# The gated-delta stage of a two-block network kernel: substitution rows by VectorE transposes, diagonal blocks in 32-partition squares, gates ahead of output tiles

## What is computed

```python
def gated_delta_rule(q, k, v, g, beta):          # chunks of 64 tokens, 16 value heads, 8 query/key heads
    g = jnp.cumsum(g, axis=-1)
    decay = jnp.exp(jnp.where(lower, g[..., :, None] - g[..., None, :], -jnp.inf))
    L = jnp.where(strict, jnp.einsum('bhncd,bhnsd->bhncs', kb, k) * decay, 0.0)
    T = lax.linalg.triangular_solve(eye + L, ..., lower=True, unit_diagonal=True)
    u = T @ vb
    w = T @ (kb * jnp.exp(g)[..., None])
    attn = jnp.einsum('bhncd,bhnsd->bhncs', q, k) * decay
    # scan over chunks: v_new = u - w @ state; o = q_dec @ state + attn @ v_new; state = state*g_last + k_dec^T @ v_new
```

## Time and profile before

| | us |
|---|---|
| median of 3 runs | 2825.57 (2825.46 to 2825.92) |
| the profiled execution | 2824.96 |
| its span, first to last instruction | 2822.8 |
| PE busy | 2751.5 (97%) |
| DVE busy | 1599.3 (57%) |
| ACT busy | 1206.9 (43%) |
| POOL busy | 633.0 (22%) |
| gated-delta stage with its projections | about 1885 to 2484 on the span's clock |

### The profile page before, as it was taken

The page is one execution under the profiler, slowest core; times in us unless marked ns, Lnnn a source line. Parts: engine busy times, 40 slices in busy tenths (PEclk is TensorE's granted clock), DMA queues, the critical chain, the costliest instruction groups (busy, mean ns, idle before and its releaser), DMA issues.

```text
span 2822.8 us, 40991 instructions
## 1 busy us (share of the span) xinstructions
PE 2751.5 (97%) x14276; PEld 2233.3 (79%) x14276; DVE 1599.3 (57%) x2460; ACT 1206.9 (43%) x1813; POOL 633.0 (22%) x602
## 2 busy tenths in 40 slices
PE   8999999999999999999999999998999999899998
PEld 6888887788888888887778888877888888677777
DVE  5444336544433675437945754257777777676664
ACT  4333242533332333224443332345555555457665
POOL 2000003100001450013633510113333333223222
PEclk9999999999999999999999999999999999999999
DMA  5333322233333564332214643322222222222222
GB/s 148 97 97 91 95 75 83 75 97 97 97 95 99 149 186 120 96 94 79 68 37 125 188 142 91 95 70 75 56 66 69 68 69 61 49 68 60 67 60 67
DMA packets 484837, 255.37 MB, mean 90 GB/s; under 512 B 17843, under 2 KB 478422, under 8 KB 484710
## 3 DMA queue, kind: packets, MB, share of 16 engines
q1 hardware_dynamic: 484534, 253.40, 31.4%
q10 hardware_dynamic: 176, 0.27, 0.0%
HBM read 251.51 MB, written 2.13 MB: 90 GB/s over the span
## 4 chain that ended last, share of the span: by engine, by line
PE 86%; DVE 6%; ACT 3%; issue 2%; POOL 1%; DMA 0%; ACTq 0%; DVEq 0%; POOLq 0%; SPq 0%
PE bank L258 68%; PE bank L1840 2%; DVE w_lo L244 1%; PE bank L1871 1%; PE bank L1944 1%; PE bank L1873 1%; PE bank L1872 1%; DVE dsa_work L1542 1%; ACT w_hi L238 1%; DVE small L1540 1%; PE bank L2748 1%; PE bank L2740 1%; POOL gdn_dn_off L2500 1%; PE bank L2773 1%; PE bank L946 1%
## 5 line engine op out<-in xcount | busy, mean ns | idle before, releaser
L258 PE MATMUL bank<-x_hi,w_hi 128*128 128x512 f32 x2320 | 940.7, 405 | 7.6 <-DVE w_lo L244 3.7
L258 PE MATMUL bank<-x_hi,w_lo 128*128 128x512 f32 x2320 | 907.8, 391 | 0.0
L258 PE MATMUL bank<-x_lo,w_hi 128*128 128x512 f32 x2320 | 907.0, 391 | 0.6 <-DVE x_lo L554 0.6
L244 DVE TENSOR_TENSOR w_lo<-w_raw,w_hi 128x1024 fp32r<-128x1024 f32 x429 | 547.9, 1278 | 561.5 <-ACT w_hi L238 561.1
L238 ACT ACTIVATE w_hi<-w_raw 128x1024 fp32r<-128x1024 f32 x429 | 450.6, 1055 | 612.9 <-PE bank L258 567.4
L258 PEld LDWEIGHTS bank<-x_hi,w_hi 128*128 128x128 f32 x2320 | 437.0, 188 | 104.9 <-issue 14.1
L258 PEld LDWEIGHTS bank<-x_hi,w_lo 128*128 128x128 f32 x2320 | 436.4, 188 | 93.3
L258 PEld LDWEIGHTS bank<-x_lo,w_hi 128*128 128x128 f32 x2320 | 437.5, 189 | 89.4 <-issue 5.7
L429 POOL TENSOR_TENSOR sumsq<-sumsq,sq 128x512 f32<-128x512 f32 x51 | 85.3, 1673 | 1285.8 <-ACT sq L415 1285.2
L258 PE MATMUL bank<-h_hi,w_hi 128*128 128x512 f32 x768 | 298.9, 389 | 1.6 <-DVE h_lo L1575 1.6
L258 PE MATMUL bank<-h_hi,w_lo 128*128 128x512 f32 x768 | 298.8, 389 | 0.0
(11 more groups left out here) (483 smaller groups left out, 3556.9 us busy)
## 6 DMA issues: line engine op xcount, KB each, us to landing
w_raw<-in_ffn_wi_dram SPq DMA_DIRECT2D x176, 512.0 KB, 3.8
w_raw<-in_ffn_wo_dram SPq DMA_DIRECT2D x64, 512.0 KB, 3.6
w_raw<-in_ada_w_dram SPq DMA_DIRECT2D x48, 512.0 KB, 4.9
w_raw<-in_a_w_in_dram SPq DMA_DIRECT2D x48, 512.0 KB, 4.0
w_raw<-in_b_w_in_dram SPq DMA_DIRECT2D x32, 512.0 KB, 4.1
w_raw<-in_ffn_wo_dram SPq DMA_DIRECT2D x32, 384.0 KB, 3.1
w_raw<-in_even_w_in_dram SPq DMA_DIRECT2D x16, 512.0 KB, 4.1
w_raw<-in_a_w_out_dram SPq DMA_DIRECT2D x16, 512.0 KB, 3.6
```

The source lines that it names most:

```text
L244: dve.tensor_tensor(w_lo[s][:], w_raw[raw_of(b) % RAW][:], w_hi[s][:].bitcast(F32), ALU.subtract).then_inc(w_lo_done, 1)
L258: mm = pe.matmul(out, lhs[:, w], rhs(kt), start=first and kk == 0 and m == 0, stop=last and kk == len(kts) - 1 and m == 2)
```

## The change

It touches the gated-delta stage alone.

- The selection matmuls and `pick` are gone. DVE transposes the 128 columns of C in 32 x 32 squares ("across"), then transposes a pattern that repeats each element 16 times into 1920 columns of SBUF ("rows"), which hold row k of each block spread over its partitions. The substitution reads its rows there, where it read PSUM banks.
- `m` is no longer 2 x (128 x 512) but four products of 32 partitions x 256 elements on the 32 x 32 squares of the diagonal, and the two reductions become one addition of two halves. POOL masks the decay likewise in four squares for both heads.
- The output norm is folded into the gate: POOL multiplies silu(z) by W5 ("zr", two products); DVE's `normed` goes.
- The two gates silu(z) are taken in the turn of their own projection, and the z blocks are ahead of Oa, Ob in the order of blocks; output tiles come late in a turn.
- "ga", "gb" go from DVE to ACT; DVE's `at_0`, `at_1` from ahead of the substitution to behind "f2b"; DVE's `low` from ahead of "va", "vb" to behind them; f2 waits for "hb".
- ACT's logarithms, roots, gate rows and decays of the next head run at t = 1 and 2; the table load for the logarithms stands at the turn's end. Splits, convolutions and output additions are moved as the tables say.

The diff, cut:

```diff
-            "mid": {"kt": "q0", "kk": "q1", "vt": "q2", "sel": "q3", "inv": "k0 k1 k2 k3 v00 v01 v02", "c": "v03", "f2": "v10", "v": "v11 v12", "y": "v13 O0",
-                    "at": "O1", "vn0": "O2", "ds0": "O3", "ks1": "O4", "vn1": "O5", "ds1": "O6", "ks2": "O7", "vn2": "z00", "ds2": "z01",
-                    "ks3": "z02", "vn3": "z03 z10", "o3": "z11 z12 z13"},
+            "mid": {"kt": "q0", "kk": "q1", "vt": "q2 q3", "inv": "k0 k1 k2 k3 v00 v01 v02", "c": "v03", "f2": "v10", "v": "v11 v12", "y": "v13 z00",
+                    "at": "z01 z02", "vn0": "z03", "ds0": "z10", "ks1": "z11", "vn1": "z12", "ds1": "z13", "ks2": "O0", "vn2": "O1", "ds2": "O2",
+                    "ks3": "O3", "vn3": "O4", "o3": "O5 O6 O7"},
-                      "mid": {"start": "q", "vc": "k", "f": "v0", "f2": "v1", "at": "Oa", "vn3": "Ob", "end": "z0 z1"},
-                      "last": {"start": "z0", "f": "z1", "f2": "Oa", "vn3": "Ob"}}
+                      "mid": {"start": "-", "PT": "q", "vc": "k", "f": "v0", "vn0": "v1", "r1": "z0", "vn2": "z1", "vn3": "Oa"},
+                      "last": {"start": "- z0", "f": "z1", "vn0": "Oa", "vn3": "Ob"}}
# gdn_pe, turn
-                for g, (out, free) in enumerate(...):
-                    dve("in_1")
-                    pe.wait_ge(*free)
-                    for k in range(4 * g, min(4 * g + 4, GDN_STEPS)):
-                        mm = pe.matmul(out[:, x], G.pick[g][:, x], G.blocks[:, 0:P], start=True, stop=True)
                 beside("inv")
                 dve("PT")
+                act("vc_1")
                 ...
-                act("fb")
-                dve("gb")
+                act("gb")
+                dve("hb")
                 halves("f2", ...)
# gdn_act, turn
                 if p is not None:
                     inverse_roots(p)            # its table load is now at the end of the turn before
                 splits("start")
 ...
-                splits("vc")
-                if p is not None:
-                    for h in range(2):
-                        gate(h, *gdn_gate(at, i, h)[:3])
+                splits("PT")
                 if more:
                     pool("qd_1")
                     conv(0, j + 1, i, at, odd)
+                    splits("vc")
                     conv(1, j + 1, i, at, odd)
 ...
+                pe("g")
+                run("ga", G.m[a, :], second(0)[a], ACT.Copy)
+                run("gb", G.m[b, :], second(1)[b], ACT.Copy)
 ...
+                    if more and t == 0:
+                        silu(2, i, at, odd)
+                        silu(3, i, at, odd)
+                        gate(0, i, at)
                     splits(f"vn{t}")
+                    splits(f"r{t}")
+                    if at.kind == "mid" and t == 1:
+                        gate(1, i, at)
                     if more and t == 1:
+                        logarithms(j + 1)
+                    if more and t == 2:
                         roots(j + 1)
                         gate_rows(j + 1)
+                        decays(j + 1)
 ...
                 if more:
-                    decays(j + 1)
-                splits("end")
+                    act.preload_act_table_set("natural_log_exp_and_others")
# gdn_dve, turn
+                for r in gdn_squares():          # four slices of 32 partitions
+                    made = dve.tensor_tensor(squares_of(G.W1[0])[r]..., first(0)[r, :]..., squares_of(G.dn_in)[r]..., ALU.mult)
+                tt("in", G.C[:, :, :], squares_of(G.W1[0])[:, :, 0:INV_BLOCK], squares_of(G.W1[0])[:, :, INV_BLOCK:2 * INV_BLOCK], ALU.add)
+                dve.transpose(G.across.rearrange("p (b k g) -> p g b k", b=2, g=4), gdn_blocks[:, 0:P]).then_inc(*done("across"))
+                dve.transpose(G.rows[:, 0:P * GDN_STEPS],
+                              G.across.rearrange("p (b x r) -> p x b r", b=2, r=1)[:, 0:4 * GDN_STEPS].to_broadcast(by_row_of_block)).then_inc(*done("rows"))
-                for h in range(2):
-                    tt(f"m_{h}", G.W1[h][:], first(0)[:], G.dn_in[h][:], ALU.mult)
-                for h in range(2):
-                    dve.tensor_reduce(G.C[:, TT * h:TT * h + TT, :], ...)
-                    tt(f"at_{h}", G.attnT[h][:], first(1)[:], G.dec[h][:], ALU.mult)
-                if p is not None:
-                    normed(p)
 ...
+                splits("PT")
                     conv(0, j + 1, i, at, odd)
 ...
-                    outs(*((0,), (2,), (5,), (7,))[t])
+                    outs(*((), (), (0,), (2,))[t])
 ...
-                    outs(*((1,), (3, 4), (6,), ())[t])
+                    outs(*((), (), (1,), (3, 4))[t])
 ...
+                if more:
+                    outs(5, 6, 7)
# gdn_pool, turn: eye first, then qdec, kdec, and new:
+                    for h in range(2):
+                        pool.wait_ge(*GdnOut.act.after(f"rs_{h}", p))
+                        pool.tensor_tensor(G.zs[h][:], G.zs[h][:], G.W5[h][:], ALU.mult).then_inc(*GdnOut.pool.done(f"zr_{h}"))
```

More of the change, by code:

```diff
@@ L1671, in __init__ @@
                 self.kind, self.m = kind, m
-                names = {"front": "q k v0 v1", "first": "q k v0 v1 z0 z1", "mid": "q k v0 v1 Oa Ob z0 z1", "last": "z0 z1 Oa Ob", "end": "Oa Ob"}[kind].split()
+                names = {"front": "q k v0 v1", "first": "q k v0 v1 z0 z1", "mid": "q k v0 v1 z0 z1 Oa Ob", "last": "z0 z1 Oa Ob", "end": "Oa Ob"}[kind].split()
                 self.b = Gdn.b0 + {"front": 1, "first": 5, "mid": 11 + 8 * m, "last": 59, "end": 63}[kind]
@@ L2119, in gdn_act @@
                 silu(u, 0, front, 0)
+            logarithms(0)
             roots(0)
@@ L2132, in inverse_roots, with gate @@
                     act.activation(G.W5[h][:], G.W5[h][:], ACT.Exp, scale=-0.5).then_inc(*O.act.done(f"rs_{h}"))
-            def gate(h, through, src, before):
-                act.wait_ge(*through)
-                act.wait_ge(*before)
-                act.activation(G.zs[h][:], src[:], ACT.Silu).then_inc(tile_free, 1)
+            def gate(h, i, at):
+                act.wait_ge(*at.through(f"z{h}", i))
+                act.wait_ge(tile_free, BANKS + at.tile[f"z{h}"] + i * 28)
+                act.activation(G.zs[h][:], at.bank(f"z{h}")[:], ACT.Silu).then_inc(tile_free, 1)
             def high(p):
@@ L2182, in turn @@
                 pe("f2")
+                if p is not None:
+                    act.wait_ge(*GdnOut.pool.after("zr_0", p))
                 run("f2a", G.F2[a, :], first(0)[a], ACT.Copy)
+                if p is not None:
+                    high(p)
                 if more:
                     conv(2, j + 1, i, at, odd)
-                if p is not None:
-                    high(p)
-                splits("f2")
                 pe("y")
@@ L2194, in turn @@
                     squares(j + 1, odd, p)
-                    conv(3, j + 1, i, at, odd)
                 else:
                     for h in range(2):
-                        gate(h, at.through(f"z{h}", i), at.bank(f"z{h}"), (tile_free, BANKS + at.tile[f"z{h}"]))
+                        gate(h, i, at)
                 pe("at")
@@ L2201, in turn @@
                 if more:
+                    conv(3, j + 1, i, at, odd)
                     sums(j + 1)
-                splits("at")
-                if more:
-                    silu(2, i, at, odd)
                 for t in range(TT):
@@ L2359, in turn @@
-                for h in range(2):
-                    tt(f"E_{h}", G.E[h][:], first(0)[:], G.dn_off[h][:], ALU.mult)
-                for h in range(2):
-                    pe("qk")
-                    dve.wait_ge(*N.act.after(f"dec_{h}", j))
-                    tt(f"at_{h}", G.attnT[h][:], first(1)[:], G.dec[h][:], ALU.mult)
-                if p is not None:
-                    normed(p)
+                    tt(f"E_{h}", G.E[h][:], first(0)[:], G.dn_off[h][:], ALU.mult)
                 for k in range(GDN_STEPS):
-                    rows = (second(1), second(0), first(0), first(1))[k // 4][:, (k % 4) * P:(k % 4) * P + P].rearrange("p (c i) -> p c i", i=INV_BLOCK)
+                    rows = G.rows[:, k * P:k * P + P].rearrange("p (c i) -> p c i", i=INV_BLOCK)
@@ L2375, in turn @@
                     else:
+                        own("rows")
                         pool("eye")
@@ L2411, in turn @@
                     tt(n, G.V[r, :], G.V1[r, :], src[r], ALU.add)
+                if p is not None:
+                    low(p)
+                splits("vc")
                 if more:
@@ L2414, in turn @@
                 splits("f")
-                if more:
-                    conv(2, j + 1, i, at, odd)
                 pe("at")
```

149 lines of the change are left out of this document (74 added, 75 removed), and 6 rows, old and new, of the table GDN_BESIDE.

## The result

The changed kernel takes 2836.11 us (median of 8 runs, 2830.40 to 2837.34), the kernel before 2825.94 us beside it: 1.0034 times as long, 95% interval 1.0025 to 1.0043. It is slower by about 10 us where 15 us were forecast to be won. The profiled execution took 2837.05 us, its span 2835.3 against 2822.8 before: 12.5 us to explain. The eight runs spread with the clock: the fastest, 2830.40 us, has a mean granted clock of 0.991, the four of about 2837 us have 0.987.

A forecast was written before the change was run, and what follows sets the result against it. TensorE was taken to set the pace. Six middle turns won 12.7 us, and with 1.6 (first turn), 0.3 (turn change) and 0.5 (last turn) 15.1 us, off the median 2825.57: 2810.5 us, range 2792 to 2825.

The forecast's parts named there:

- The 3.34 us a middle turn of the selection: TensorE's selection matmuls go, 3.34 us a turn; eight turns make 26.7 us.
- The wide transpose: VectorE's transpose of 1920 columns ahead of the substitution takes 2.2 us, bounds 2.0 and 5.6.
- rival 2: The wide transpose is slow, 5.6 us instead of 2.2, each turn loses 3.4: 2837.7 us; chance 0.08.
- rival 3: GpSimd's two new products block two substitution steps by 1.3 us each, 2.6 a turn: 2828.7 us; chance 0.08.
- The wait of 0.57 us ahead of the first output matmul: TensorE's wait, released by ScalarE, ends as splits "at" and "end" move: 0.57 us a turn.
- The wait ahead of z00: VectorE's low splits and z0 split contend with GpSimd behind vb; TensorE waits 1.0 us, bounds 0 and 2.5.
- The sum: Middle turn: 4.82 us won, less 1.7 of waits ahead of f and f2 and 1.0 ahead of z00: 2.1 us.
- the add "in": VectorE's add of 128 elements ahead of the substitution: 0.3 us, plus about 0.6 us waiting beside GpSimd's kd.
- VectorE's bound of the middle turn: VectorE's chain limits the first turn, leaving 2.8 us of its 3.34 + 2.02; that turn wins 1.6 us in all.
- f comes 2.2 us earlier: Last turn: f starts 2.2 us earlier, where TensorE already waited 2.58 us for the transpose; 0.5 us won in all.
- the first output tile: Last turn: it now waits for "low" behind va and vb, counted within the turn's gain of 0.5 us.
- Rival 4: Rearranged splits or the load ring stall TensorE 1 to 2 us more each turn: 2817 to 2825 us; chance 0.14.

The follow-up runs named there:

- experiment 6: Changed kernel with five changes of order (products, GpSimd's front, low, start splits, Silu) and fillers in first and last turn: 2805.82 us, 0.9929.
- Experiment 1: Changed kernel with filler matmuls in the wait ahead of f, 15 in the first turn, 7 in each middle, 32 in the last: 2826.52 us, 1.0005.
- experiment 9: Experiment 6's kernel without its filler matmuls in the first and last turn: 2810.86 us, 0.9946.
- experiment 4: Changed kernel with GpSimd's front for the next head waiting for at, behind VectorE's low splits, not for vb: 2829.98 us, 1.0013.
- experiment 10: Changed kernel with experiment 2's shifted products and experiment 4's later GpSimd front together, nothing else: 2817.48 us, 0.9968.
- experiment 2: Changed kernel with product v03 moved ahead of f and later products one place earlier in each middle turn: 2830.79 us, 1.0017.
- experiment 7: Kernel before with four further VectorE transposes between P and the last transpose, 512 columns in middle turns, 32 in end turns: 2848.73 us, 1.0083.
- Experiment 5: Changed kernel with VectorE's low put back ahead of va and vb in the last turn alone: 2833.36 us, 1.0025.
- experiment 3: Kernel before with only the two VectorE transposes in place of the selection matmuls and their pick: 2859.85 us, 1.0124.
- experiment 8: Experiment 7's kernel with nine filler matmuls ahead of f in the middle turns: 2848.65 us, 1.0085.

## Why the prediction was wrong

The forecast was a gain of 15.1 us in the profiled execution; it lost 12.5, 27.6 us apart. By parts: the first turn was to win 1.6 and lost 6.4 (8.0 apart); the six middle turns with the turn change were to win 13.0 and won 0.5 (12.5); the last was to win 0.5 and lost 6.9 (7.4). (The three make 27.9; the rest lies outside the stage.)

**What held.** The 3.34 us a middle turn of the selection are the right size (experiment 6: 66.85 us of work left). The wide transpose took 2.18 us, forecast 2.2; the doubt about its repeated source, rival 2, fell. The nine microseconds from the first step to the transpose of P did not change: the lock of rival 3 didn't touch the steps there (2138.32 to 2147.57, 9.25 us). The wait of 0.57 us ahead of the first output matmul went. The wait ahead of z00 came with the named mechanism, 0.6 us instead of 1.0.

**The step that failed: a wait was priced at its length.** The sum took 1.7 us for f and f2 and nothing for what a wait does to the clock. The kernel before had no wait ahead of f in its middle turns and a clock of 1.00 there; its last turn had 2.58 us at 0.97. Experiment 1 measures what this costs in the six middle turns: 2.2 + 4.5, together 6.6 of the 12.5 us that are apart there. Behind f in the end turns TensorE was busy 2.9 us longer in the first, with 7 matmuls fewer (35.69 against 32.74, clock 0.87 against 1.00), and 3.8 us longer in the last for the same 325 (33.50 against 29.66, clock 0.81 against 0.95). How much of that the waits ahead of f alone caused isn't shown: fillers there gave back nothing in the first turn and 0.5 us in the last in the changed kernel (experiment 1), 1.1 and 1.9 in the order of experiment 6 (experiment 9).

**Sizes in the middle turn: the other 5.9 us.** At full clock it took 70.83 us, not 69.5. The waits ahead of f and f2 are 1.90 and 0.34 us, where the sum had 1.7 for both, and 0.47 ahead of v, where ScalarE's copies were taken as in time. The transpose of P ended 17.1 us behind kk, forecast 16.6: the low split of v0 took 1.90 us and not 1.23, as VectorE ran it beside GpSimd's qdec and kdec. I had taken GpSimd as idle there and put the meeting, with 0.6 us, on the add "in", which took 0.37; and the four squares took 1.72, not 1.4, because such small operations start 0.43 us apart. A wait of 0.37 us ahead of vn3, for a split beside GpSimd, was not in the sum, and TensorE's work was 67.16 us, 0.3 more than 66.85. These 0.3 stand at the wait ahead of z00: without it two matmuls there overlap and the first of z00 takes 0.39 us, behind it they don't overlap and it takes 0.50. They are absent where that wait is gone (66.82 and 66.86 us in experiments 4 and 10) and present in experiment 2 (67.20). With z00's wait of 0.59 in place of 1.0 the terms add up: 1.0 - 0.4 + 0.4 + 0.3 = 1.3 us, which is 70.83 less 69.5.

**First turn: the gain hung on a step of another engine.** I let VectorE's bound of the middle turn stand for the first. There GpSimd still makes its masks inside the turn; its four narrow ones ended at 1923.05 and VectorE had waited 4.08 us for them. f then waited 4.14 us, where it had not waited; the selection had waited 2.02. From k's transposes to f it was 24.11 us, where it had been 24.35: 0.2 won of the 2.8 that I had reckoned. Of the 6.4 us that the turn ended late, 1.9 stand ahead of k's transposes (23.44 us behind 1892.29, before 21.51); they come with the half clock at its start, which kernels without the change show too (experiment 7). The other 4.7 stand behind f: 2.9 of busy time, as said, and 1.8 of waits. TensorE waited 1.83 us ahead of v for f2a, which stands behind a table load and a Silu of ScalarE, and 1.59 ahead of y for VectorE's vb; before, it had been 1.61 ahead of v. Rival 3's lock did show once here: the first step took 1.00 us, not 0.27, beside GpSimd's kdec.

**Last turn: the moved splits.** I wrote that f comes 2.2 us earlier. It came 24.10 us behind the turn's first sum (2437.43 less 2413.33), where it was 24.21. The two start splits, now straight ahead of the squares and beside GpSimd, took 3.90 us, so that the squares began 8.45 us behind the sum where m had begun 7.31 behind it. That ate what the reductions gave. TensorE, with less to do, waited 8.12 us in place of 2.58. Then the first output tile waited 2.87 us; I had named that wait and priced it within a net gain of 0.5. Behind f the turn took 7.05 us longer: 3.8 of busy time at the lower clock and 3.2 of waits. Experiment 5 won 1.65 us back, and the fillers another 1.9 in experiment 6.

**The rivals.** None gives what happened. Rival 4 (splits stall TensorE elsewhere) is the kind of the misses in size, 1.3 us a turn, but it was bounded at 2825. The range ended below the result, since both things that carried it over, the clock and the two end turns, had been given no unfavourable bound.

**Slips that change nothing.** The terms given for ScalarE behind f add up to 7.6 us, not 7.5. The turn of 71.67 us repeats five times, not six (one of the five took 71.82): the first of the six middle turns took 74.84, as the row above shows.

## What to carry over

Where one engine sets the pace and another's chain ends close behind it, taking work from the first shows the second's chain in full. In such a case cost the chain of the other engine first, and the work saved only up to it; experiment 3 lost 34 us with a "free" saving of 3.34 us a turn. A wait of TensorE in a dense stretch costs its length and can cost the clock behind it too, so give it a second, unfavourable term. Two late steps in one turn must be tried together: alone, either may give little or nothing, as experiments 2, 4 and 10 show. And the first and the last turn of a pipeline need their own sums: 15 of the 27.6 us apart lie in those two. Last, look at the clock of a stretch that the change doesn't touch before comparing two profiles: here 1.9 us of the first turn's loss began there.

## What the runs showed of the hardware

An idle time of 1.90 to 1.94 us ahead of f was followed by matmuls at half clock in four of five like turns of the changed kernel, and in three of five in experiment 5, where these turns are the same; one of 2.44 to 2.53 us in experiment 7 in two of five; those of 6.6 to 8.4 us in experiment 3 in all five. One of 0.54 to 0.72 us (experiments 2, 6, 9 and 10) was never followed by it, nor were the two of 1.39. One of 1.75 to 1.80 us at the start of the first turn was in seven of twelve profiles. Where the clock fell, a turn of the changed kernel mostly lost 0.6 to 0.8 us (in two of seven cases 2.1), with GpSimd later (experiment 4) 0.7 to 1.8; the matmuls of f, g and c in the stretch shown were 1.45 us longer. Fillers held the clock in the middle turns, and in part in the ends (experiments 1, 8, and 6 against 9).

A VectorE transpose of 1920 columns whose source reads each element 16 times took 2.18 us, 1.14 ns an element, against 1.39 for the one of 512 (0.71 us): no cost of the repeated read shows. From 512 to 1920 columns the time grew by 1.04 ns an element. The Trainium skill says of the transpose mode that it sustains one element per cycle per lane (page "Vector Engine (DVE) Microarchitecture Reference", section 3.8); the rows agree in so far as the time follows the elements written, and don't show how long a cycle is.
